# Expert stage: token rows moved as four pieces on four partition quarters and transposed by VectorE, in and out

## The reference

```
scores = sigmoid(h @ router_w)                   # h = rms_norm(x, norm_ffn), 32 experts in 8 groups
best group by its two highest biased scores, then the top 2 experts in it; gate weights sum to 1
a = xs @ w_gate[e]; u = xs @ w_up[e]             # 1024 -> 512
y = (silu(a) * u) @ w_down[e]                    # 512 -> 1024
x = x + sum over the token's 2 experts of gate * y
```

## Time and profile before

| | |
|---|---|
| median of 3 runs | 3923.0 us (3918.75 to 3928.27) |
| profiled execution | 3918.82 us |
| its span, first to last instruction | 3917.0 us |
| TensorE busy | 3779.1 us, 96% |
| VectorE, ScalarE, GpSimd busy | 1240.5, 664.6, 583.9 us |
| DMA | 587.32 MB, mean 150 GB/s |
| expert stage, first layer (first gate/up matmul to last down matmul) | 1056.6 to 1953.0 us |
| expert stage, second layer | 3010.6 to 3906.2 us |

### The profile page before, as it was taken

How to read it: one execution, slowest core, us unless ns; L and a number is a source line. 1 busy time by engine, 2 the same in 40 slices (tenths; PEclk the granted TensorE clock), 3 DMA queues, 4 the chain that set the end, 5 groups by cost and what they waited for, 6 DMA issues and landing times.

```text
span 3917.0 us, 60762 instructions
## 1 busy us (share of the span) xinstructions
PE 3779.1 (96%) x21748; PEld 2804.6 (72%) x21748; DVE 1240.5 (32%) x4460; ACT 664.6 (17%) x1796; POOL 583.9 (15%) x842
## 2 busy tenths in 40 slices
PE   8999999999699999999989999999996999999998
PEld 4555555555499999999945555555554999999998
DVE  3555555554200100111035555555542000010100
ACT  1212212121011111111112122121210111111111
POOL 1010110101011112111110101101010111121211
PEclk9999999998699999999989999999987999999999
DMA  5110101102277788879831101011022777878796
GB/s 203 49 42 32 49 24 49 45 29 88 96 235 235 239 267 264 276 259 317 280 108 49 36 37 49 24 49 42 31 94 94 233 235 258 266 250 290 259 318 197
DMA packets 240658, 587.32 MB, mean 150 GB/s; under 512 B 26460, under 2 KB 26716, under 8 KB 240220
## 3 DMA queue, kind: packets, MB, share of 16 engines
q1 hardware_dynamic: 215228, 508.33, 35.6%
q0 software_dynamic: 25152, 75.59, 8.5%
HBM read 510.38 MB, written 74.58 MB: 149 GB/s over the span
## 4 chain that ended last, share of the span: by engine, by line
PE 95%; DVE 2%; issue 1%; DMA 1%; DVEq 0%; ACT 0%; SPq 0%; ACTq 0%; POOL 0%; POOLq 0%
PE bank L1250 26%; PE bank L1045 23%; PE bank L1282 14%; PE bank L1190 11%; PE bank L1020 10%; PE bank L1140 2%; PE bank L1139 2%; PE bank L1110 2%; PE bank L1129 1%; PE bank L1169 1%; PE bank L1128 1%; PE bank L1091 1%; PE bank L1099 0%; PE bank L1153 0%; PE bank L1118 0%
## 5 line engine op out<-in xcount | busy, mean ns | idle before, releaser
L1250 PE MATMUL bank<-arena,wts 128*128 128x136 f32 (+6 forms) x8192 | 1050.6, 287 | 1.6 <-DVE arena L989 1.6
L1250 PEld LDWEIGHTS bank<-arena,wts 128*128 128x128 f32 x8192 | 1026.5, 191 | 3.4 <-issue 1.8
L1045 PE MATMUL bank<-wts,arena 128*128 128x512 f32 x2048 | 968.4, 626 | 3.6 <-DVEq L756 3.6
L1045 PEld LDWEIGHTS bank<-wts,arena 128*128 128x128 f32 x2048 | 401.9, 203 | 458.9 <-issue 455.0
L1020 PE MATMUL bank<-cst,arena 128*128 128x128 f32 (+10 forms) x2944 | 477.2, 278 | 78.5 <-DVE arena L748 32.0
L1282 PE MATMUL bank<-arena,wts 128*128 128x136 f32 (+6 forms) x4096 | 549.4, 290 | 0.0
L1282 PEld LDWEIGHTS bank<-arena,wts 128*128 128x128 f32 x4096 | 514.1, 190 | 4.3
L1020 PEld LDWEIGHTS bank<-cst,arena 128*128 128x128 f32 (+10 forms) x2944 | 352.4, 136 | 210.4 <-issue 90.5
L1190 PE MATMUL bank<-wts,arena 128*128 128x512 f32 x1024 | 453.9, 597 | 1.9 <-DVE arena L832 1.9
L998 DVE TENSOR_TENSOR arena<-arena,bank 128x136 f32<-128x136 f32 (+6 forms) x64 | 19.5, 304 | 1239.3 <-ACT arena L684 1239.3
L1190 PEld LDWEIGHTS bank<-wts,arena 128*128 128x128 f32 x1024 | 193.9, 192 | 235.3 <-issue 235.3
(11 more groups left out here) (161 smaller groups left out, 2756.2 us busy)
## 6 DMA issues: line engine op xcount, KB each, us to landing
wts<-in_w_gate SPq DMA_DIRECT2D x128, 1024.0 KB, 8.3
wts<-in_w_up SPq DMA_DIRECT2D x128, 1024.0 KB, 10.9
wts<-in_w_down SPq DMA_DIRECT2D x128, 1024.0 KB, 11.0
hrows<-arena SPq DMA_DIRECT2D x34, 512.0 KB, 3.0
out<-arena SPq DMA_DIRECT2D x34, 512.0 KB, 2.6
arena<-in_x SPq DMA_DIRECT2D x32, 512.0 KB, 4.8
wts<-in_w_in SPq DMA_DIRECT2D x8, 2048.0 KB, 16.0
arena<-out SPq DMA_DIRECT2D x32, 512.0 KB, 4.6
```

What stands on the lines that cost most here:

```text
L1045: i = mm(bIP[n % 2][:, :], hT[:, d], win[:, n, d], start=(d == 0), stop=(d == DC - 1))
L1250: return mm(gu_at(f, k, w), lhs, xT[:, d, 0:w], start=start, stop=(d == DC - 1), skip_group_check=True)
```

## The change

Rows in `hrows` and `out` are now seen as four pieces of 256 values. The table holds 4 x token. A quarter of the partitions (32 of them) holds one piece number: partition 32a + s holds piece a of token s of a group. A group is up to 32 tokens, G = ceil(w / 32) groups per expert, and the widths 152, 148 and 136 become 155, 150 and 135, so that a group has w / G tokens. Partitions without a token point at spare rows.

- SyncE loads the table four times, once for each quarter.
- GpSimd adds the quarter's number (one `tensor_tensor`) and issues G gathers of 1 KB per partition, and later G adds. `xg`, `ysb` and `xT` are double.
- VectorE transposes each 32x32 block from `xg` to `xT` (one instruction and a drain per group), then multiplies `xT` by the norm weights. On the way back three transposes read the down result from PSUM and write `ysb`. TensorE transposes nothing in this stage.
- ScalarE scales `ysb` in place, once per group, and no longer copies the down result.
- Feature order changes with it: partition p now holds features 8p to 8p + 7. The gate and up weights are loaded as runs of 4 x 512 values per partition and half; the down weights keep their place in SBUF but are read by TensorE with a step of 8 between columns.
- TensorE waits for `xT_ready` before an expert and for `y_turned` of the expert before ahead of the down matmuls.

```
-WIDTHS = (NT,) * 6 + (160,) * 2 + (152,) * 2 + (148,) * 3 + (140,) * 3 + (136,) * 8 + (P,) * 8
+WIDTHS = (NT,) * 6 + (160,) * 2 + (155,) * 2 + (150,) * 3 + (140,) * 3 + (135,) * 8 + (P,) * 8
+GROUPS = tuple(-(-w // 32) for w in WIDTHS)
+GMAX = max(GROUPS)
+PIECE = D // 4
-PADS = 256
+PADS = 512
...
+        def windows(tile, at, n, stride, w):
+            g = -(-w // 32)
+            step = w // g
+            first = tile[:, at:at + 32]
+            return bass.AP(first.tensor, first.offset, [first.ap[0], [stride, n], [step, g], [1, 32]])
...
-                            src = w[bass.ds(l, 1), bass.ds(i, 1), g * 512:(g + 1) * 512, :]
+                            src = w[bass.ds(l, 1), bass.ds(i, 1), :, :].rearrange("o u (p d) f -> p (o u d) f", d=DC)
                             e.dma_start(wexp[:, b, g, k * 2048:(k + 1) * 2048].rearrange("p (d f) -> p d f", d=4),
-                                        src.rearrange("o u (d p) f -> p (o u d) f", p=P)).then_inc(w_full[g][b], 16)
+                                        src[:, 4 * g:4 * g + 4, :]).then_inc(w_full[g][b], 16)
...
-                        e.dma_start(tab0[:, 2 * i:2 * i + 2], table[bass.ds(slot, P), :]).then_inc(tab_full[b], 16)
-                        if w > P:
-                            e.dma_start(tab1[0:w - P, 2 * i:2 * i + 2], table[bass.ds(slot + P, w - P), :]).then_inc(tab_full[b], 16)
+                        g = GROUPS[i]
+                        for a in range(4):
+                            e.dma_start(tab[32 * a:32 * a + w // g, i, 0:g, :], table[bass.ds(slot, w), :].rearrange(
+                                "(g s) c -> s g c", g=g)).then_inc(tab_full[b], 16)
...
-                            wait_alone(e, gathered, (turn * TURN_BLOCKS + blocks_to(1)) * 16)
+                            wait_alone(e, x_turned, h * 2 + 1)
...
+                        wait_alone(e, tab_full[b], h * 64 + (i // 2 + 1) * 64)
+                        e.tensor_tensor(piece[:, i, 0:GROUPS[i]], tab[:, i, 0:GROUPS[i], 0], quarter[:, 0:GROUPS[i]], ALU.add)
+                        e.drain()
+                        if i >= 2:
+                            wait_alone(e, x_turned, h * 2 + i - 1)
+                        for g in range(GROUPS[i]):
+                            e.indirect_dma_start(xg[b][:, g * PIECE:(g + 1) * PIECE], None, hpieces, bass.IndirectOffsetOnAxis(
+                                ap=piece[:, i, g:g + 1].bitcast(U32), axis=0)).then_inc(gathered[b], 16)
                     def add(i, b, w):
+                        for g in range(GROUPS[i]):
+                            wait_alone(e, y_scaled, turn * TURN_GROUPS + groups_to(i) + g + 1)
+                            e.indirect_dma_start(opieces, bass.IndirectOffsetOnAxis(
+                                ap=piece[:, i, g:g + 1].bitcast(U32), axis=0), ysb[b][:, g * PIECE:(g + 1) * PIECE], None,
                                 compute_op=ALU.add).then_inc(added, 16)
-                        wait_alone(e, added, (turn * TURN_BLOCKS + blocks_to(i + 1)) * 16)
+                        wait_alone(e, added, (turn * TURN_GROUPS + groups_to(i + 1)) * 16)
...
+                    def y_scale(i, b):
+                        e.wait_ge(y_turned, h * 2 + i + 2)
+                        for g in range(GROUPS[i]):
+                            y = ysb[b][:, g * PIECE:(g + 1) * PIECE]
+                            a(y, y, ACT.Copy, scale=tab[:, i, g, 1:2].bitcast(F32)).then_inc(y_scaled, 1)
...
+                    def x_in(i, n, b, w):
+                        xT = xT_at(b, w)
+                        e.wait_ge(gathered[b], (turn * LANE_GROUPS[b] + lane_groups_to(i)) * 16)
+                        if i >= 2:
+                            e.wait_ge(gu_done, n * 2 + 2)
+                        step = w // GROUPS[i]
+                        for g in range(GROUPS[i]):
+                            x_piece = xg[b][:, g * PIECE:(g + 1) * PIECE].rearrange("p (r d) -> p d r", d=DC)
+                            v.transpose(windows(xT_all[b], g * step, DC, 32 * GMAX, 32), x_piece)
+                            e.drain()
+                        e.nop().then_inc(x_turned, 1)
+                        v.tensor_tensor(xT, xT, bc(gffn8.unsqueeze(2), [P, DC, w]), ALU.mult).then_inc(xT_ready, 1)
+                    def y_turn(i, n, b, w):
+                        e.wait_ge(down_done, n + 3)
+                        if i >= 2:
+                            e.wait_ge(x_adds, n)
+                        g = GROUPS[i]
+                        for k, bk in enumerate((bF, bIP0, bIP1)):
+                            m = 3 if k < 2 else 2
+                            y = ysb[b][:, 0:g * PIECE].rearrange("p (g r d) -> p d g r", g=g, d=DC)
+                            v.transpose(y[:, 3 * k:3 * k + m], windows(bk, 0, m, w, w))
+                        e.drain().then_inc(y_turned, 1)
                     def expert(i, half, b, w):
+                        if i >= 1:
+                            y_turn(i - 1, n - 1, 1 - b, WIDTHS[i - 1])
+                        if i < NE - 1:
+                            x_in(i + 1, n + 1, 1 - b, WIDTHS[i + 1])
                         e.wait_ge(silu_done, n * 3 + 1)
...
-                        e.wait_ge(xT_read, n * 4 + 4)
+                        e.wait_ge(xT_ready, n + 1)
...
+                        e.wait_ge(y_turned, n + 1)
                         wait_alone(e, w_full[2][b], (h + half + 1) * 32)
...
-                                lhs = wexp[:, b, 2, f * D + d * P:f * D + d * P + P]
+                                lhs = wexp[:, b, 2, f * D:f * D + D].rearrange("p (m d) -> p d m", d=DC)[:, d]
```

More of the change, by code:

```diff
@@ L35 @@
 NT = 168
-WIDTHS = (NT,) * 6 + (160,) * 2 + (152,) * 2 + (148,) * 3 + (140,) * 3 + (136,) * 8 + (P,) * 8
-BLOCKS = tuple(1 + (w > P) for w in WIDTHS)
-TURN_BLOCKS = sum(BLOCKS)
-LANE_BLOCKS = tuple(sum(BLOCKS[b::2]) for b in range(2))
+WIDTHS = (NT,) * 6 + (160,) * 2 + (155,) * 2 + (150,) * 3 + (140,) * 3 + (135,) * 8 + (P,) * 8
+GROUPS = tuple(-(-w // 32) for w in WIDTHS)
+TURN_GROUPS = sum(GROUPS)
+LANE_GROUPS = tuple(sum(GROUPS[b::2]) for b in range(2))
+GMAX = max(GROUPS)
+PIECE = D // 4
 ROUNDS = -(-SEQ // NT)
 STRIDE = ROUNDS * NT
-PADS = 256
+PADS = 512
 EPS = 1e-6
@@ L45 @@
 FIRST = 4096
-ARENA = 25024
+ARENA = 25016
 WINDOWS = (2, 4, 8, 16)
@@ L135, in program @@
     table = nc.dram_tensor("table", (NE * STRIDE, 2), I32).ap()
+    hpieces, opieces = (t.rearrange("t (a c) -> (t a) c", a=4) for t in (hrows, out))
     with ExitStack() as ctx:
@@ L169, in program @@
         rb = par[:, 412:444]
+        gffn8 = par[:, 444:452]
         qgs = sb("qgs", 1)
         base = sb("base", 32)
-        count = sb("count", 4)
         rounds = sb("rounds", 1, I32)
[L174 to L178, removed]
+        tab = sb("tab", NE * GMAX * 2, I32)[:, :].rearrange("p (i g c) -> p i g c", i=NE, g=GMAX)
+        quarter = sb("quarter", GMAX, I32)
         order = sb("order", 32, I32)
-        cur = [sb(f"cur{b}", 4, I32) for b in range(2)]
-        rows_in = [sb(f"rows_in{b}", 2, I32) for b in range(2)]
         stat = sb("stat", 64)
@@ L227, in program @@
         pay = [sb(f"pay{b}", 4, I32) for b in range(2)]
-        xg = part("moe", 2 * D).rearrange("p (k d) -> p k d", k=2)
-        xT_all, sgm_all, hTm_all, yTs_all = (part("moe", n * NT) for n in (DC, FC, FC, DC))
-        ysb = part("moe", 2 * D).rearrange("p (k d) -> p k d", k=2)
+        xg, ysb = ([part("moe", GMAX * PIECE) for _ in range(2)] for _ in range(2))
+        xT_all = [part("moe", DC * 32 * GMAX) for _ in range(2)]
+        sgm_all, hTm_all = (part("moe", FC * NT) for _ in range(2))
+        piece = part("moe", NE * GMAX).bitcast(I32).rearrange("p (i g) -> p i g", i=NE)
         consts_full, pad_rows = sem("consts_full"), sem("pad_rows")
@@ L240, in program @@
         tab_full = [sem(f"tab_full{b}") for b in range(2)]
-        slots_written, gathered, added = sem("slots_written"), sem("gathered"), sem("added")
+        slots_written, added = sem("slots_written"), sem("added")
+        gathered = [sem(f"gathered{b}") for b in range(2)]
         sumsq_f, hn_ready, pe_hnT, hT_ready = sem("sumsq_f"), sem("hn_ready"), sem("pe_hnT"), sem("hT_ready")
@@ L982, in _ @@
                     h = e.snap(halves)
-                    def x_in(n, w):
-                        xT = at_width(xT_all, w)
-                        for k in range(4):
-                            e.wait_ge(pe_xT, n * 4 + k + 1)
-                            v.tensor_tensor(xT[:, 2 * k:2 * k + 2], (bA, bB)[k % 2][:, 0:2 * w].rearrange("p (d n) -> p d n", d=2),
-                                            bc(gffn[:, 2 * k:2 * k + 2].unsqueeze(2), [P, 2, w]), ALU.mult).then_inc(xT_read, 1)
-                    x_in(h * 2, WIDTHS[0])
+                    turn = e.snap(turns)
+                    def x_in(i, n, b, w):
[7 more added lines that the diff above has]
+                            v.transpose(windows(xT_all[b], g * step, DC, 32 * GMAX, 32), x_piece)
```

(4 more changed lines are left out.)

148 lines of the change are left out of this document (35 added, 113 removed).

## The result

The changed kernel takes 4147.2 us (median of 4 runs, 4145.0 to 4153.3) against 3925.6 (4 runs): 1.0567 times as long, 95% interval 1.0544 to 1.059. The forecast was 3705, the range ended at 3900. The profiled execution took 4145.0, its span is 4143.2.

What follows compares the result with a forecast made beforehand. TensorE, busy 96% of the span, was taken as the bound, with DMA next. Terms -273.0 + 1.2 + 17.0 + 37 = -218 took the median 3923 to 3705 us; own range 3655 to 3760, with the first rival to 3900.

Steps and rivals of the forecast that it cites:

- Strided weight loads: ... I take no change: TensorE's down-weight reads at a step of 8 elements (32 bytes): no added time, with the slower case left to a rival.
- The second rival: Strided weight loads set the down part's pace, 0.223 us per instruction; +408 us for both layers, 4076 us; chance 0.18.
- The break-even: Down-weight load length at which the change gains nothing against 3923: 0.185 us, 1.66 times the present pace.
- The transposes that leave TensorE: Expert stage: all TensorE transposing between experts goes, 136.5 us a layer, -273.0 for two; new widths add 1.2.
- The ends of a layer: Expert stage's start and end, where TensorE waits anyway: +5.0 and +3.5 us a layer, +17.0 for two.
- The DMA term: Widths 140 and 135: DMA load of 24.0 us per expert exceeds the matmuls; +37 us for both layers.
- the third rival: Transposes gone but x late from table or gathers; each microsecond beyond slack costs 64; within the first rival's range.
- 4 us of slack: Next expert's x: transposes end 11 us into an expert, before VectorE is next needed at 14.3 + 0.5.
- VectorE's transposes: 32x32-block transposes moved to VectorE: 0.4 us for 256 elements, between 0.27 and 0.85, not on the path.
- The first rival: Fetch and return path (GpSimd turn or DMA load) bounds nearly everywhere; +168 us in place of 37, 3836; chance 0.24.

Runs made afterwards that it cites:

- E2: The kernel before the change with only its down weights read at a step of 8 columns; 4399.6 us.
- E3: The changed kernel with the four quarters of the down part reading weights at steps of 1, 2, 4 and 8 floats; 3907.9 us.
- E4: The changed kernel with down-weight quarters read at steps of 3, 5, 16 and 32 floats and VectorE's transposes reading and writing adjacent columns; 4018.8 us.
- E10: E8 with each expert's four table loads issued one expert earlier; 3666.1 us, ratio 0.935 to the kernel before the change.
- E1: The changed kernel with down weights read in adjacent columns again, output permuted; 3699.7 us, ratio 0.9425 to the kernel before the change.
- E9: E1 with half of each expert's down weights not fetched; 3688.1 us, ratio 0.9419 to the kernel before the change.
- E8: E5 with the load of the down weights requested earlier; 3692.7 us, ratio 0.9418 to the kernel before the change.
- E5: The changed kernel with ScalarE copying each expert's down weights into adjacent columns for TensorE; 3701.3 us, ratio 0.9431 to the kernel before the change.
- E7: E1 with gate and up weights loaded in 2 KB runs as before the change; 3709.7 us, ratio 0.9469 to the kernel before the change.

## Why the prediction was wrong, step by step

**The step that failed is "Strided weight loads: ... I take no change".** The second rival came true. Per layer, 64 x (32 x 0.2388 - 757.2 / 192) = 236.7 us where I took 0, 473 for both; E2 measures 475 by itself. The rival's own price was low, 408, since I took twice the pace of width 128 (0.223) and the loads follow each other at 0.2388: the difference is 64 x 32 x 0.0158 x 2 = 65 us, and 4076 + 65 = 4141 against 4147 measured. The break-even that the prediction gave, a load of 0.185 us or 1.66 times the pace, was passed by far (2.1 times).

What I had in hand spoke for the rival and not for "no change". The trace of before had no strided load, so nothing in it excluded a loss, while the earlier trace rows and the pace at width 128 showed that the loads are the limit there, with nothing to hide a slower one. The right treatment of an edit with a price between 0 and over 408 us in a sum of -218 is to let it decide the forecast; I left it at its lower end without a reason.

E3 bears out the rule that I had cited: two columns per 16 bytes (step 2) run at full pace, one (steps 4 and 8) at 0.239. The Trainium skill ("Advanced Engine Details and Errata", SBUF Cachelines) says just this of a line and its two hits. E4's step 3, 128 values in 96 such lines, lies between. The 0.21 and 0.22 of steps 5, 16 and 32 are also far above full pace, but the rule as cited doesn't say why they are below 0.239, and no run shows it.

**The transposes that leave TensorE** (-273.0, and +1.2 for the widths): right. With full pace and full supply a layer's stage should be 757.2 + 3.2 of the lower clock = 760.4 us, and E10 has 761.5 with 1.1 of waits; before it was 896.3. In after it is 757.2 + 236.7 + 3.2 + 3.7 of waits = 1000.8, measured 1000.94.

**The ends of a layer** (+17.0): measured +14.5. In the first layer the start, from the ready number of rounds (1037.81 in after) to the first matmul (1059.78), takes 22.0 us where it took 17.6, so +4.4 for my +5.0; the end, from the last down matmul (2060.72) to the reload of x (2073.69), takes 13.0 where it took 10.9, so +2.1 for my +3.5. In the second layer the start is +4.1. Its end is the end of the run: from the last down matmul (4128.42) to the last instruction 14.8 us, before 10.8, so +3.9. The second layer's expert stage, of before and of after:

```profile
3010.57:3906.16 895.59, 895.56 (x7016) 858.90 (x7016) 86.25 (x220) 140.46 (x300) 153.29 (x215) 1.00 0.78 259
...
3127.93:4128.42 1000.49, 997.45 (x6144) 997.03 (x6144) 248.25 (x372) 93.17 (x250) 409.35 (x337) 1.00 0.75 236
```

The account of after is then 104.6 + 104.9 for the stages and 14.5 for their ends, 224.0 of the 226.2 us between the spans. The other 2.2 lie in the mix stages (-1.3 and +3.4), and I haven't followed them.

**The DMA term** (+37): too large, and for the wrong reason. In E1 TensorE waits 27.1 us for the products, 8.0 of them in the first experts of the layers, where I had put no wait; so 19.1 stand against my 37. That E1 comes within 5 us of the forecast is in part luck. I had derived it from a load of 24.0 us per expert at five groups. The shares agree with that: in after, gathers and adds take 24.8% and the weights 55.2% of the DMA engines at a period of 30.0 us, 7.4 and 16.6 us where I had 7.8 and 16.2. But that sum is no floor. E10 moves the same bytes at width 135 in 22.1 us per expert with TensorE never idle, at a DMA share of 1.02. E9, with 1 of 6 MB gone, still waits 10.0 in its first layer. What holds TensorE is above all the chain of 23.0 us that E9 shows, which E10 broke by its first link; it is the third rival: x is late. The DMA engines' load has some part in the waits, since E9 waits less than E1; through which step isn't shown (the fetch that lands ahead of the wait at 1540 us in E1 and at 1539 in E9 takes 7.3 us in both). I had given it 4 us of slack; the fetch took 17.7 us (1515.9 to 1533.6) where I had 14.9, mostly a landing of 7.3 us in place of 4.1, and 5.3 from landing to product where I had 4. In after it doesn't show, since the down part has grown to 15.3 us.

**VectorE's transposes**: 645 ns and 1038 for 256 and 480 elements where I took 400 ns for 256, which measured inside the bounds of 270 and 850; E4 shows that the step costs a third of both. GpSimd: 0.97 us for a gather and 1.66 for an add with gaps of 0.30, as I had it (1.02, 1.63, 0.3).

**The first rival** (the fetch and return path bounds nearly everywhere, 3836) is out as a price: E1, with that path unchanged, takes 3700.

## What to carry to other kernels

A new access pattern of an operand is an edit of its own, with a price per instruction: count the instructions that read it before looking at what the pattern saves elsewhere, and when the trace has no row of it, forecast with its bad end. Where an engine must read with a step, let one with idle time do it once and write the result adjacent. A queue in order turns a late fetch for the next item into a wait of the present one; requesting the small table one item ahead took 27 us off the run (0.9418 to 0.935, E8 to E10).

## What the runs showed of the hardware that I had not expected

- TensorE's 128-column float32 weight loads follow each other at 0.112 us at steps of 1 and 2 floats, 0.18 at 3, 0.239 at 4 and 8, 0.21 at 5, and 0.22 at 16 and 32: not the farthest but steps 4 and 8 are slowest. Why they differ by 0.02 is open.
- VectorE pays in its 32x32 transposes: 645 ns at a read step of 8 and 446 adjacent for 256 elements (after, E4). ScalarE seems to pay in the same way: 2060 ns for 1024 elements read at step 8, against 1057 in a row that is adjacent but writes bfloat16 (E5).
- A DMA share near 1 doesn't mean that no more can be moved. At a share of 1.00 E1 moves 335 GB/s, E10 moves 341 in the same stretch at 1.02, and in one window of E3 a share of 1.01 stands beside 426.
- The same bytes in 8 KB in place of 2 KB runs gained 10 to 17 us of 3700, with TensorE's waits 7.0 us shorter (E7 against E1).
